# Recurrent mixer: step sizes in two passes, the diagonal scored with the neighbours, first convolution taps on ScalarE, GpSimd's differences in five places

## The reference, cut to what matters

```python
def recurrent_mixer(h, w_in, conv_w, conv_b, dt_bias, a_log, d_skip, ssm_norm, g_norm, lb, w_out):
    proj = h @ w_in
    z, xbc, dt, hq, hf, hi, hg = split_cols(proj, [...])
    xbc = silu(causal_depthwise_conv_2(xbc, conv_w, conv_b))        # 4 taps, 1024 channels
    xs, b_in, c_in = split_cols(xbc, [512, 256, 256])
    dt = softplus(dt + dt_bias)                                      # the step sizes: 8 heads
    y = ssd_chunked(xs, dt, -exp(a_log), b_in, c_in)
    ...
    log_f = logaddexp(log(lb), log1p(-lb) + log_sigmoid(hf))
    k_in = (1 - lb) * sigmoid(-hf)
    q = silu(hq)
    o = hgrn2_chunked(q, k_in, hi, log_f)                            # 4 heads of 128
    ...
    return concatenate([y, o], -1) @ w_out

# in hgrn2_chunked: G is the running sum of log_f over the tokens
scores[t, s] = sum over k of q[t, k] * exp(G[t, k] - G[s, k]) * k_in[s, k]    for s <= t
```

## Time and profile before

| what | value |
|---|---|
| runs | 949.22, 3311.82, 948.82 us |
| median | 949.22 us |
| the profiled execution | 948.97 us, its span 947.2 us |
| TensorE busy | 931.3 us (98%) |
| VectorE, ScalarE, GpSimd busy | 682.9 (72%), 519.5 (55%), 92.4 us (10%) |
| granted TensorE clock, mean | 0.998 |
| 16 DMA engines | 167.00 MB, mean 176 GB/s |

### The profile page before, as it was taken

The page is one execution under the profiler, slowest core; times in us unless marked ns, Lnnn a source line. Parts: engine busy times, 40 slices in busy tenths (PEclk is TensorE's granted clock), DMA queues, the critical chain, the costliest instruction groups (busy, mean ns, idle before and its releaser), DMA issues.

```text
span 947.2 us, 12949 instructions
## 1 busy us (share of the span) xinstructions
PE 931.3 (98%) x5213; PEld 810.5 (86%) x5213; DVE 682.9 (72%) x920; ACT 519.5 (55%) x710; POOL 92.4 (10%) x111
## 2 busy tenths in 40 slices
PE   8999999999999999899999999999999999999997
PEld 7998888888888898788888888889998888888885
DVE  5899857666667977866766666568999767666663
ACT  6887545444546667964544434468685545334432
POOL 2550200000011100100000000000243010000000
PEclk9999999999999999999999999999999999999999
DMA  9933665665545454146656555556423457656531
GB/s 291 346 129 124 195 231 205 199 201 194 205 135 200 130 172 176 45 134 222 216 190 206 177 190 179 177 158 215 140 91 111 134 161 249 212 179 199 176 114 44
DMA packets 106955, 167.00 MB, mean 176 GB/s; under 512 B 2896, under 2 KB 82848, under 8 KB 106768
## 3 DMA queue, kind: packets, MB, share of 16 engines
q1 hardware_dynamic: 104688, 158.23, 51.2%
q0 software_dynamic: 2208, 7.95, 2.4%
HBM read 165.13 MB, written 1.05 MB: 175 GB/s over the span
## 4 chain that ended last, share of the span: by engine, by line
PE 83%; DVE 10%; ACT 5%; issue 1%; DMA 1%; POOL 0%; DVEq 0%; ACTq 0%; POOLq 0%
PE ps L399 80%; DVE wl L1950 3%; PE ps L407 2%; DVE SC L2588 1%; ACT wh L1333 1%; DVE SC L2081 1%; DMA raw<-in_s_w_in 1%; ACT SC L1665 1%; ACT junk L1321 1%; DVE fs L2091 0%; DMA h<-in_x 0%; ACT SC L1737 0%; DVE SC L2582 0%; DVE SC L2066 0%; DVE SC L2595 0%
## 5 line engine op out<-in xcount | busy, mean ns | idle before, releaser
L1950 DVE TENSOR_TENSOR wl<-raw,wh 128x2048 fp32r<-128x2048 f32 (+2 forms) x141 | 317.9, 2258 | 142.9 <-ACT wh L1333 142.8
L1333 ACT ACTIVATE wh<-raw 128x2048 fp32r<-128x2048 f32 (+2 forms) x150 | 281.9, 1885 | 156.5 <-PE ps L399 138.4
L399 PE MATMUL ps<-xhl,wh 128*128 128x512 f32 (+1 forms) x1248 | 254.7, 350 | 0.3 <-ACT wh L1402 0.3
L399 PEld LDWEIGHTS ps<-xhl,wh 128*128 128x128 f32 x1248 | 199.3, 190 | 26.8 <-issue 0.7
L399 PE MATMUL ps<-wh,xhl 128*128 128x512 f32 (+3 forms) x800 | 190.5, 380 | 0.0
L399 PEld LDWEIGHTS ps<-wh,xhl 128*128 128x128 f32 x800 | 142.7, 188 | 24.7
L399 PEld LDWEIGHTS ps<-xhl,wl 128*128 128x128 f32 x1008 | 135.7, 191 | 7.5
L399 PE MATMUL ps<-xhl,wl 128*128 128x256 f32 x1008 | 140.6, 282 | 0.0
L399 PE MATMUL ps<-wl,xhl 128*128 128x512 f32 (+3 forms) x403 | 102.1, 375 | 0.2 <-DVE wl L1964 0.2
L399 PE MATMUL ps<-wh,fh 128*128 128x512 f32 x304 | 91.0, 392 | 0.3 <-DVE fl L2319 0.3
L399 PE MATMUL ps<-wh,fl 128*128 128x512 f32 x304 | 90.2, 389 | 0.0
(11 more groups left out here) (295 smaller groups left out, 835.6 us busy)
## 6 DMA issues: line engine op xcount, KB each, us to landing
raw<-in_ffn_gate SPq DMA_DIRECT2D x22, 1024.0 KB, 5.4
raw<-in_ffn_up SPq DMA_DIRECT2D x22, 1024.0 KB, 5.5
raw<-in_ffn_down SPq DMA_DIRECT2D x22, 1024.0 KB, 4.9
raw<-in_w_up SPq DMA_DIRECT2D x16, 1024.0 KB, 5.5
raw<-in_w_down SPq DMA_DIRECT2D x16, 1024.0 KB, 5.0
raw<-in_s_w_in SPq DMA_DIRECT2D x14, 1024.0 KB, 5.4
raw<-in_w_in SPq DMA_DIRECT2D x9, 1024.0 KB, 9.8
raw<-in_a_w_in SPq DMA_DIRECT2D x6, 1024.0 KB, 5.3
```

The source lines that it names most:

```text
L399: return e.matmul(o, a, b, start=start, stop=stop, skip_group_check=True)
L1333: e.activation(high_of(i), raw_of(i), ACT.Copy).then_inc(*up("act_high", i))
L1950: e.tensor_tensor(low_of(i), raw_of(i), high_of(i).bitcast(F32), ALU.subtract).then_inc(*up("dve_lo", i))
```

## The change

1. *Step sizes in two passes.* High and low weights stand beside each other in one stationary tile `wdt_hl`, so that rows 0 to 7 of a product hold the high part's and rows 64 to 71 the low part's result; TensorE makes two passes (xh and xl) in place of three. ScalarE copies rows 64 to 71 out, VectorE adds them with the bias. The low weights are made ahead of VectorE's `lows` and not behind them.
2. *Diagonal with the neighbours.* At level 7 (blocks of two) the even key and query stay as they are and only the odd ones are weighed, in place, the key by exp(G_even - G_odd), the query by its inverse. The product of hk and hq then holds the neighbours' scores and the diagonal at once. `score(8)` goes from TensorE's and VectorE's lists; the mask of level 7 takes in the diagonal and its selection covers all columns; GpSimd zeroes `STt` beforehand, ahead of two DMAs in its queue.
3. *First taps on ScalarE*, behind the `highs` of each i and ahead of `conv_silu(i - 1)`; VectorE keeps the other three taps.
4. *Differences in five places*: levels 0 to 4 have each their own, levels 5, 6 and 7 reuse those of 2, 0 and 1.
5. The two row copies into `T3` move from ScalarE to GpSimd, and VectorE's `dve_dt_turned` moves ahead of `conv(0)`.

```diff
-        wdt_h, wdt_l = (sb(n, [128, 184], F32R) for n in ("wdt_h", "wdt_l"))
+        wdt_hl = sb("wdt_hl", [128, 184], F32R)
...
+        differences = (Dd[:, 0, :], Dd[:, 1, :], Dd[:, 2, :], grow[:, 1, :], junk[:, :], Dd[:, 2, :], Dd[:, 0, :], Dd[:, 1, :])
...
-                for n, (w, x) in enumerate(((wdt_h, xh), (wdt_h, xl), (wdt_l, xh))):
-                    if n != 1:
-                        e.wait_ge(*(at("dve_dt_low") if n else at("act_dt_high")))
+                e.wait_ge(*at("dve_dt_low"))
+                for x in (xh, xl):
                     for k in range(8):
 
-                        d = mm(ps[0][:, 0:256], w[:, 8 * k:8 * k + 128], x[:, k, :], n == 0 and k == 0, n == 2 and k == 7)
+                        d = mm(ps[0][:, 0:256], wdt_hl[:, 8 * k:8 * k + 128], x[:, k, :], x is xh and k == 0, x is xl and k == 7)
                 d.then_inc(*up("pe_dt"))
...
-                        if n == 8:
-                            e.wait_ge(*at("act_hq", 1))
-                        elif n == 1:
+                        if n == 1:
                             e.wait_ge(*at("dve_cb", tb))
                         elif n == 2:
-                            e.wait_ge(*at("dve_score", 8, tb))
+                            e.wait_ge(*at("act_hq", 1))
...
+                    elif n == 7:
+                        score(n, hk, hq)
...
-                e.wait_ge(*at("dve_keys", 3))
-                score(8, hk, hq)
...
+                e.wait_ge(*at("pe_dt"))
+                e.activation(dr[R, 1, :], ps[0][64:72, 0:256], ACT.Copy).then_inc(*up("act_dt_part"))
...
-                    if i == 1:
-                        e.wait_ge(*at("pool_seg_rest"))
-                        for n, x in enumerate((middle, rest)):
-                            e.activation(T3[32 + 32 * n:40 + 32 * n, :], x[R, :], ACT.Copy).then_inc(*up("act_seg_rows", n))
+                    e.wait_ge(*at("act_xbc", i))
+                    for t in (2 * i, 2 * i + 1):
+                        e.activation(xb[:, t, :], xf[:, t, :], ACT.Identity, scale=P("cw", 4 * t + 3)).then_inc(
+                            *up("act_conv_tap", t))
...
+                e.wait_ge(*at("act_dt_high"))
+                e.tensor_tensor(wdt_hl[:, 64:128], wdt, wdt_hl[:, 0:64].bitcast(F32), ALU.subtract).then_inc(*up("dve_dt_low"))
                 lows(S["hi"][0] + 4)
-                e.wait_ge(*at("act_dt_high"))
-                e.tensor_tensor(wdt_l[:, 0:64], wdt, wdt_h[:, 0:64].bitcast(F32), ALU.subtract).then_inc(*up("dve_dt_low"))
                 R = slice(0, 8)
-                e.wait_ge(*at("pe_dt"))
-                e.tensor_scalar(dr[R, 0, :], ps[0][R, 0:256], P("dtb")[R], None, ALU.add).then_inc(
+                e.wait_ge(*at("act_dt_part"))
+                e.scalar_tensor_tensor(dr[R, 0, :], ps[0][R, 0:256], P("dtb")[R], dr[R, 1, :], ALU.add, ALU.add).then_inc(
                     *up("dve_softplus", "dt", "x"))
...
-                    for t in both:
-                        e.tensor_scalar(xb[:, t, :], xf[:, t, :], P("cw", 4 * t + 3), None, ALU.mult).then_inc(
-                            *up("dve_conv_tap", t, 3))
-
                     for k in (2, 1, 0):
                         for t in both:
-                            e.wait_ge(*at("dve_conv_tap", t, k + 1))
+                            e.wait_ge(*(at("act_conv_tap", t) if k == 2 else at("dve_conv_tap", t, k + 1)))
...
-                conv(0)
                 e.wait_ge(*at("pe_dt_turned"))
                 for tb in range(2):
                     o = ps[0][:, 128 * tb:128 * tb + 128]
                     e.tensor_scalar(At[:, tb, 0:8], o[:, 0:8], -1.0, None, ALU.mult)
                     d = e.tensor_copy(At[:, tb, 32:40], o[:, 32:40])
                 d.then_inc(*up("dve_dt_turned"))
+                conv(0)
...
-                    i = 7 if n == 8 else n - 1
                     for tb in range(2):
                         v = ps[LEVEL_BANK[n][tb]][:, :].rearrange("p (h n) -> p h n", h=4)
-                        mk, z = hm[:, i, :].unsqueeze(1).to_broadcast([128, 4, 128]), STt[:, 4 * tb:4 * tb + 4, :]
+                        mk, z = hm[:, n - 1, :].unsqueeze(1).to_broadcast([128, 4, 128]), STt[:, 4 * tb:4 * tb + 4, :]
                         e.wait_ge(*at("pe_score", n, tb))
-                        if n == 8:
-                            e.tensor_tensor(z, v, mk, ALU.mult).then_inc(*up("dve_score", n, tb))
-                        else:
-
+                        if n < 7:
                             z, v, mk = (x.rearrange("p h (s i n) -> p h s i n", i=2, n=LEVELS[n - 1])[:, :, :, 1, :] for x in (z, v, mk))
-                            e.wait_ge(*(at("dve_score", n - 1, tb) if n > 3 else at("act_score", 2, tb)))
-                            e.copy_predicated(z, mk.bitcast(I32), v).then_inc(*up("dve_score", n, tb))
+                        e.wait_ge(*(at("dve_score", n - 1, tb) if n > 3 else at("act_score", 2, tb)))
+                        e.copy_predicated(z, mk.bitcast(I32), v).then_inc(*up("dve_score", n, tb))
...
-                    d4, o4 = (x.rearrange("p (b i m) -> p b i m", i=2, m=m) for x in (Dd[:, n % 3, :], QK[:, n % 2, :]))
-                    if n >= 2:
-                        e.wait_ge(*at("pe_score", n - 2, 1))
+                    d4, o4 = (x.rearrange("p (b i m) -> p b i m", i=2, m=m) for x in (differences[n], QK[:, n % 2, :]))
                     e.wait_ge(*at("act_decay", n))
-                    e.tensor_tensor(o4, kq, d4, ALU.mult).then_inc(*up("dve_weighed", n))
+                    if n == 7:
+
+                        odd = SC[:, 0:2048].rearrange("p (i b j) -> p b i j", i=2, j=2)[:, :, :, 1]
+                        e.tensor_tensor(odd, odd, differences[n].rearrange("p (b i) -> p b i", i=2), ALU.mult).then_inc(
+                            *up("dve_weighed", n))
+                    else:
+                        if n >= 2:
+                            e.wait_ge(*at("pe_score", n - 2, 1))
+                        e.tensor_tensor(o4, kq, d4, ALU.mult).then_inc(*up("dve_weighed", n))
...
+            e.memset(STt, 0.0).then_inc(*up("pool_zero_scores"))
             e.dma_start(wdt, D["s_w_in_2"][:, 1536:1544].rearrange("(k p) n -> p k n", p=128)).then_inc(*up("dma_wdt"))
             e.dma_start(hm, D["hmask"]).then_inc(*up("dma_hm"))
...
+            e.wait_ge(*at("pool_seg_rest"))
+            for n, x in enumerate((middle, rest)):
+                e.tensor_copy(T3[32 + 32 * n:40 + 32 * n, :], x[R, :]).then_inc(*up("pool_seg_rows", n))
+                e.wait_ge(*at("pool_seg_rows", n))
...
-                if n >= 3:
-                    e.wait_ge(*at("dve_weighed", n - 2))
-                e.tensor_tensor(d3[:, :, 0:m], ref, g3[:, :, 0:m], ALU.subtract)
+                if n >= 5:
+                    e.wait_ge(*at("dve_weighed", {5: 2, 6: 0, 7: 1}[n]))
+                e.tensor_tensor(d3[:, :, 0:m], ref, g3[:, :, 1:2] if n == 7 else g3[:, :, 0:m], ALU.subtract)
...
-    hm[:, 7, :] = np.eye(128)
+    hm[:, 6, :] += np.eye(128, dtype=f)
```

More of the change, by code:

```diff
@@ L48 @@
                       "act_exp act_map_turned act_latent_out act_back"),
-    "act_recurrent": ("act_bound act_xs act_score act_seg_rows act_dt_high act_hq act_forget act_keys act_log_forget act_rate act_z act_hi act_decay act_between "
+    "act_recurrent": ("act_bound act_xs act_score act_dt_high act_dt_part act_conv_tap act_hq act_forget act_keys act_log_forget act_rate act_z act_hi act_decay act_between "
                       "act_xbc act_hg act_xb act_xs act_cb act_seg act_gated_square act_silu"),
@@ L1786, in recurrent @@
                 e.wait_ge(*at("pool_zero_dt_pad"))
-                e.activation(wdt_h[:, 0:64], wdt, ACT.Copy).then_inc(*up("act_dt_high"))
+                e.activation(wdt_hl[:, 0:64], wdt, ACT.Copy).then_inc(*up("act_dt_high"))
                 def z_silu(tb):
@@ L1839, in decay @@
                     e.wait_ge(*at("pool_parted", n))
-                    e.activation(Dd[:, n % 3, :], Dd[:, n % 3, :], ACT.Exp).then_inc(*up("act_decay", n))
+                    e.activation(differences[n], differences[n], ACT.Exp).then_inc(*up("act_decay", n))
                 def seg(i):
@@ L2716, in recurrent @@
                 decayed(1)
+                weigh(2)
                 e.wait_ge(*at("dma_hm"))
-                score(8)
-                weigh(2)
                 for i in range(2, 8, 2):
@@ L2842, in gpsimd @@
             e.dma_start(pT, D["pT"].rearrange("(k p) n -> p k n", p=128)).then_inc(*up("dma_pT"))
-            e.memset(wdt_h[:, 64:184].bitcast(F32), 0.0)
-            e.memset(wdt_l[:, 64:184].bitcast(F32), 0.0).then_inc(*up("pool_zero_dt_pad"))
+            e.memset(wdt_hl[:, 128:184].bitcast(F32), 0.0).then_inc(*up("pool_zero_dt_pad"))
             e.tensor_copy(sel[:, :, :], P("sel", 0, 8).unsqueeze(2).to_broadcast([128, 8, 128])).then_inc(*up("pool_sel"))
```

12 lines of the change are left out of this document (6 added, 6 removed).

## The result

The changed kernel takes 951.92 us (median of eight runs, 951.44 to 952.67) against 949.33 for the kernel before: a ratio of 1.0028, with a 95% interval of [1.0019, 1.0037]. (One of the eight runs of before took 3311.82 us; the medians are not touched by it.) That is 2.6 us slower; I forecast 1.7. The profiled execution took 951.44 us, its span 949.6, against 948.97 and 947.2.

What follows compares the result with a forecast made beforehand. TensorE, busy 98%, was taken as the bound, but level(0) waits on ScalarE's row behind conv(3): +0.41, -2.89 and +4.2 gave about +1.75 there, +1.7 at the end; 948.97 + 1.7 = 950.7 us, range 947.0 to 952.5.

Steps and rivals of the forecast that it cites:

- TensorE's removed work: Eight step-size products (-0.98 us) and the diagonal's scores (-1.86 us) leave TensorE, together -2.84 us.
- Is level(0) ready then?: Check at level(0): weigh(0) waits for ScalarE's queries(1), so with all else unmoved only 0.7 of 2.84 us is had.
- Step a: Step sizes: ScalarE's added copy of the low part makes the scans end 0.41 us later.
- Edits at nothing: Remaining small edits, such as zeroing the scores and moving two row copies to GpSimd, were forecast to cost nothing.
- Step b: Convolutions: moving the first taps to ScalarE takes 2.89 us off VectorE.
- two covers: ScalarE's first taps for conv(0) and conv(3) are ready 0.9 us before VectorE comes to them.
- Step c: Convolutions: five GpSimd differences in one go take turns with VectorE by whole instructions, +4.2 us on VectorE.
- the walk: Main case, instruction by instruction: conv(3) ends at 688.0, +1.75 us, and the end is +1.7 us; chance 0.50.
- Plain sharing: Rival: GpSimd slows all VectorE work by 2.6 instead of turns, -0.6; with no weigh(4) wait 949.3 us; chance 0.17.
- The first rival: Convolutions gain: GpSimd's fourth and fifth differences do not delay VectorE, -1.8 us, 947.2 us; chance 0.18.
- The clock falls: Rival: TensorE's 2.9 us wait ahead of level(0) halves the clock for some 4 us of products, 954.7 us; chance 0.04.
- From there to the end: Behind conv(3): level(0) +1.1, level(1) 1.5 late, level(4) waits for weigh(4) until 710.3; +1.7 us at 712.

Runs made afterwards that it cites:

- b2: Kernel before with only the diagonal scored at level 7, three difference places; 1.0008 of the kernel before.
- b3: Kernel before with only the two-pass step sizes, low part copied by ScalarE; 1.0005 of the kernel before.
- e3: Changed kernel with the step sizes' low part copied by VectorE instead of ScalarE; 1.0024 of the kernel before.
- h2: Kernel before plus two-pass step sizes with VectorE's copy and the level 7 diagonal; three places, third difference held until conv(3) is done; 0.9996 of the kernel before.
- e4: Changed kernel with the first taps back on VectorE; 1.0049 of the kernel before.
- e1: Changed kernel with the differences in three places again; 1.0005 of the kernel before.
- g1: Changed kernel with three difference places and GpSimd's first three differences held until conv(3) is done; 1.0037 of the kernel before.
- b1: Kernel before with only the differences moved to five places; 1.0039 of the kernel before.
- e2: Changed kernel with 16 TensorE products, results unused, ahead of level(0); 1.0017 of the kernel before.
- h1: g3 with five difference places, third to fifth differences held until conv(3) is done; 1.0002 of the kernel before.
- g3: Changed kernel with three places, third difference held until conv(3) is done, ScalarE's taps ahead of highs, low part copied by VectorE; 0.9990 of the kernel before.
- g2: Changed kernel with three difference places and 14 TensorE products, results unused, ahead of level(0); 0.9993 of the kernel before.

## Why the prediction was right, and where it was not

**TensorE's removed work is not gained: shown.** b2 and b3 take away 1.86 and 0.98 us and gain 0.08 and -0.15. "Is level(0) ready then?" was the right question.

**Step a: +0.46 in place of +0.41**, by the table load (4.18 behind the first product against 3.72; e3 has it at 3.64).

**Edits at nothing: one of them was not.** I put the two row copies on GpSimd (0.4 each) at nothing because nothing is queued behind them. I looked only for who waits for them, not at whom they hinder. The copy of 657.41 takes 2.54: it starts with VectorE's subtraction and ends 0.26 behind it, and VectorE's two instructions that follow take 0.94, where they took 0.73 (0.72 in h2, which has the copies on ScalarE). That is the difference between +0.67 and a. Up to hg's slot I found no cost of the other edits.

**Step b: right in kind.** e4 loses 2.48 without it. Of the two covers, forecast at 0.9 us each, conv(0)'s is 1.1 thick (ScalarE's pair ends at 665.47, VectorE comes at 666.56). conv(3)'s held by 0.1 only: the pair ends at 686.18, VectorE comes at 686.29, halfway through the row of 683.92. Where GpSimd's turns are fewer it is gone, and conv waits 0.90 for ScalarE in e1, 3.31 in g1.

**Step c: shown.** From the first tap to conv(3)'s end the after kernel needs 22.37 (46.70 - 24.33); the walk had 688.0 - 665.67 = 22.33. e1, b1 and g1 each move it as turn-taking says. By the Trainium skill, SBUF — State Buffer, "Who interferes with whom", a two-input VectorE instruction contends with a GpSimd instruction that reads SBUF; g1's 2.44 against 7.25 agrees. Plain sharing (the "cancelled" rival) is out: conv(1) ends 15.44 behind the scans (681.72 - 666.28), where turns gave 15.43 and sharing 14.83. The first rival, convolutions gain, is out too: with fewer GpSimd instructions it is what e1 shows.

**The mis-sized term: the clock.** "The clock falls" had 4 in 100 and a price of 4 us. It happened, and costs 1.2 us at levels 0 and 1 (4.36 against 3.19 in e2; level(1) ends 2.90 later than before, where 1.5 was forecast and e2 has 1.49) and 0.8 in the end (e2). My argument against it was that no wait on operands was over 1.1 us; that told what had not been tried, and not that a longer one was safe. The price was too high since I let it last for 4 us of products, and it lasted for three microseconds of time (in g1 and h1 for more than six).

**From there to the end: a total that is near for another reason.** I forecast a wait for weigh(4) at level(4). In the changed kernel there is none: from 702.20 to 714.30 TensorE is busy without a gap. weigh(4) does end within 0.1 of level(4)'s start (at 711.17), but TensorE comes there at the same time by its own work: 2.90 late behind level(1), 2.54 late at level(4), as a short wait of the kernel before is gone. VectorE's chain is late by the clock too: weigh(2) waits 0.63 for the slowed level 0 to free its buffer, and GpSimd's sixth to eighth differences wait for weigh(2). With the clock up (e2) the wait by turns is real, but it is 0.50 at level(3), for weigh(3); level(4) is then 1.77 late where 1.96 was forecast, and hg's slot 1.39 late where it was 1.7. So without the fall the walk would have been 0.3 too high at the end, with it the stretch is 0.46 above it. That the forecast of 1.7 lies this near to the measured 2.16 is partly luck: the clock, left out, and the turns behind level(0), put too high, partly cancel.

**Open.** What lowers the clock is not settled. In the profiled executions it fell at level(0) behind waits of 2.09 to 2.77 and stayed at 1.00 behind 1.43 to 1.55 (there or at score(8)). But the same kernel may have it in one execution and not in another, as the mean clocks of b1, e1 and h1 suggest, and the moment moves: in the changed kernel the clock fell 0.4 us before level(0) began, in e3, behind the same wait of 2.77, 0.7 us after. It stayed up in e4 too, where TensorE had waited 2.71 us further up, ahead of the products of c and b:

```profile
689.40:692.00 2.60, 0.00 (x0) 0.00 (x0) 2.60 (x7) 0.88 (x3) 0.00 (x0) 1.00 0.25 101
692.00:694.00 2.00, 1.92 (x13) 1.83 (x14) 2.00 (x2) 1.98 (x5) 0.00 (x0) 1.00 0.00 0
```

(busy time as above, in e4). So the length of the last wait alone doesn't decide. What the products around it do may matter too, which no run tests: in e4 full work stood on both sides of that wait, at level(0) there are a shorter wait (0.66 in the changed kernel) and a few short products ahead of it. Why the mixer starts up to 2 us later in some profiles (641.60 to 643.63) is open as well.

## What to carry to other kernels

Before a GpSimd instruction is moved or added, write down what VectorE does in that time: beside instructions with two SBUF inputs each one cost VectorE most of its own length here (four more of 1.04 us alone cost 2.9 us by conv(3)'s end in b1), and a held GpSimd instruction may not get its turn at all. Work taken from the busiest engine is worth what the engine that feeds its next wait lets through; find that engine first, and look what the new idle time does to the clock. A small copy counts as a neighbour too, not only as a step in a chain.

## What the runs showed of the hardware

- *Turns.* Six taps of 128x255 take 2.44 us alone and 7.25 with GpSimd at work, one for each GpSimd instruction of about 1.2 us.
- *No turn.* A GpSimd instruction of 1.04 us took 6.34 (g1) and 6.43 (h2) behind four back-to-back VectorE instructions of 0.7 to 2.3 us, and ended when VectorE came to a copy out of PSUM. In the changed kernel one took 3.18, behind a single subtraction of 128x2048; in g3 one took 3.02, till VectorE idled for 0.39. Why it gets a turn between taps and not between those is not settled.
- *A small copy.* A bfloat16 copy of 8x256 on GpSimd took 2.54 us beside VectorE's subtraction of 128x2048 (0.4 for its like), and the two VectorE instructions behind it 0.94 in place of 0.73.
- *The clock.* In six profiled executions it fell to half around TensorE waits of 2.09 to 2.77 us ahead of level(0), and 24 records took 4.36 to 5.49 us in place of 3.19. With products whose results nobody uses in that wait it stayed at 1.00 (e2, g2). Not every execution of a kernel has the fall.
